# A two-layer hybrid decoder on one core: reordered work ahead of the first retrieval turn, the depthwise convolution on VectorE, and seven slots for rows of U

## The chip, the cores and the metric

One core of one Trainium2 chip runs the whole program in one launch. The metric is the device time of one execution in microseconds, here the median of the runs shown. All data is float32.

## The reference

Two layers act on x of 256 tokens by 1024. Each has two sub-layers with a post-norm residual, x <- LayerNorm(alpha x + (1 + gate) f(x (1 + scale) + shift)); scale, shift and gate come from silu(c) @ w_ada + b_ada, six vectors of 1024 per layer.

```python
proj = h @ w_in[l]                       # 1024 -> 1440, split into seven parts
o_mla  = mla_attention(...)              # 8 heads, low-rank q and kv, rotary key
o_conv = conformer_conv(conv_u, ...)     # GLU, depthwise conv over 31 taps, LayerNorm, silu, pointwise
o_swa  = swa_attention(...)              # window of 128, 4 query heads
mix = concatenate([o_mla, o_conv, o_swa]) @ w_o[l]
...
q = h @ w_pq                             # PEER: 8 heads, two halves of 128
s1, i1 = top_k(scores half 1, 16); s2, i2 = top_k(scores half 2, 16)
top_s, pos = top_k(all 256 sums, 16)     # 16 of 16384 experts per token and head
a = gelu(einsum('bqd,bqkd->bqk', xb, u_tab[e]))
y = einsum('bqk,bqkd->bqd', softmax(top_s) * a, v_tab[e])
```

The convolution is causal: for each of 256 channels, out[s] = b_dw + sum over k of h[s - 30 + k] w_dw[k].

## The kernel before

Tokens are in two blocks of 128, so there are four blocks of work, numbered m = 0 to 3 (two layers of two). Each block has eight turns, one per PEER head, and a turn has sixteen items: for item k, every one of the 128 tokens gathers its k-th row of U (4 KB each, one indirect DMA of 0.524 MB) and its k-th row of V. That makes 32 turns, 512 gathers of U and 512 of V, all issued by GpSimd in one order: U of item n + 16, then V of item n - 4.

Time is laid out by hand in **slots**. A slot is one item: slot 16 i + k is turn i, item k, and negative slots lie before the first turn. Each engine's program is a set of generators that yield the slot at which their next piece is due; `in_slot_order` (L193) merges them in slot order, and each engine's main loop runs its turn work and then everything due up to the present slot. Block m's mixing (projection, attention, convolution, output projection, norm) starts at slot BASE[m] = -140, 0, 132, 260, so that block 0's mixing lies before the first turn and each later one beside the turns of the block before. An engine does its work strictly in this order, so an early wait holds up all that is behind it.

What the change and the steps of the prediction touch:

- **U and V rows.** `ring` has UR = 6 slots for U and VR = 8 for V (L72, L235). `gather_u` (L653) waits until VectorE has used the row that was in its slot six items ago; `gather_v` (L665) waits for TensorE. VectorE's `product` (L1262, instruction L1268) multiplies a row of U by the token's own row and sums it; TensorE's `weigh` (L1707, L1721) adds rows of V into the output, weighted. Before the first turn the ring also holds pieces of w_ada, w_in and w_o.
- **Picks.** VectorE's `picks` (L1199) finds the sixteen experts of a turn in eight parts, one in each of the first eight slots of a turn, so that those slots are heavier than the last eight. The first gather waits for the picks of turn 0.
- **Query.** TensorE computes a turn's query (L1666), turns it (L1675) and computes the scores (L1685); ScalarE copies each out (L940, L945, L952).
- **Convolution.** ScalarE writes a diagonal matrix of one tap's weights (L903, `cdiag`, nine buffers) and TensorE multiplies the shifted input `hc` by it, adding in PSUM (L1609): 31 taps by 2 halves of the channels, 62 steps a block, three steps per slot from slot b + 31.2 on (b is BASE[m]). The bank "cv" is held from 31.2 to 53.3. VectorE then takes statistics (L1197), ScalarE normalises (L917) and applies silu (L921), TensorE does the pointwise product (L1623).
- **Modulation of layer 0.** w_ada is loaded in twelve chunks of 512 columns, two halves of 1 MB each (L500, L505). TensorE multiplies them (`products_of`, L1363), ScalarE copies the row (L718), TensorE turns it into columns (L1378).
- **Modulation of layer 1.** Chunks 0 to 6 are summed by VectorE (`summed`, L476: L486 for the first of eight, L491 for the others), at slots from SUM_START, and turned into columns by TensorE (L1397) at COLUMN_SLOT; chunks 7 to 11 are multiplied by TensorE at SECOND_SLOT (L1390) and their rows copied by ScalarE (L728). GpSimd waits for the sums of chunk 6 before the first gather, for the product of chunk 9 before the fifth, and for all columns before the first gather of V.
- **Loads.** SyncE issues all weights in slot order. A load waits until its buffer is free: `startup` (L544) loads chunks 4 and 5 of layer 0 (L553) ahead of the last two of the eight pieces of w_in (L556), then chunks 6 and 7. The pieces are win_load (L507).
- **End of block 0's mixing.** TensorE's output projection (L1577) is followed by VectorE's use of it (L1185, slot 74) and statistics (slot 75), the turning of sub-keys on TensorE (L1637, slots 75 and 76), ScalarE's norm (L704 to L708, slot 76.75), its turning (slot 77), the input of the query (L878).
- **Rowmax.** At slot b + 45 VectorE reduces the scores of all heads (L1151); ScalarE's exponentials (L843) wait for that and TensorE's turning of them (L1533, slot b + 48) waits for those.
- **hc** is cleared or shifted for a new block by VectorE (L1098) and ScalarE (L811), after all steps of the block before (`diag_used`).

## Time and profile before

| | |
|---|---|
| runs | 1712.57, 1715.56, 1716.38 us (median 1715.56) |
| the profiled execution's own time | 1710.71 us |
| its span | 1708.8 us |
| granted TensorE clock, mean | 0.856 |
| TensorE matmul busy | 1214.5 us, 71% |
| VectorE busy | 1063.2 us, 62% |
| GpSimd busy | 981.5 us, 57% |
| ScalarE busy | 412.9 us, 24% |

Busy time is the union of an engine's instructions. In views that list stretches, the DMA share is the mean busy share of sixteen DMA engines, so that a value just over 1 is a full one. In lists in order of time a row gives start, duration, engine, line and operation, and in brackets the idle time before it and what ended that. Work before about 200 us is that ahead of the first turn.

### The profile page before, as it was taken

Reading aid. Unit: us, or ns where it says so; the run is one execution under the profiler, and the core shown is the slowest. Engines: PE = TensorE matmul, PEld = TensorE weight load, DVE = VectorE, ACT = ScalarE, POOL = GpSimd, SP = SyncE. Lnnn points to the kernel's source line nnn. Section 1 sums busy time; section 2 is a strip of 40 time slices with the busy share of each in tenths; the row PEclk is TensorE's granted clock in tenths of the full one; section 3 lists DMA queues with packets and bytes.
Section 4 is the critical chain, followed back from the end, with each engine's and each line's share of the span. In section 5 each row is a group of like instructions: output and inputs, shape, how many; then the busy total and the mean of one; then the engine's idle time right before and its main releaser. Section 6 shows DMA issues by size and latency. Waiting matters only on the chain.

```text
span 1708.8 us, 16190 instructions
## 1 busy us (share of the span) xinstructions
PE 1214.5 (71%) x5018; PEld 544.5 (32%) x5018; DVE 1063.2 (62%) x3052; ACT 412.9 (24%) x1000; POOL 981.5 (57%) x1044
## 2 busy tenths in 40 slices
PE   6887749789766667798665567798866665666554
PEld 2465523355222222354221222355322221222111
DVE  0165486577666566577576566577766686667652
ACT  1362302454121012354031012355120020011000
POOL 2000166567666566567566566566766666667763
PEclk8997859999977779899988788899988887778789
DMA  9989999999999999999999999999999999999996
GB/s 364 342 307 352 344 400 405 405 404 409 407 398 405 410 395 403 404 403 388 404 402 406 410 391 403 405 394 342 409 405 405 405 405 407 406 408 409 410 409 235
DMA packets 217190, 667.12 MB, mean 390 GB/s; under 512 B 21586, under 2 KB 50611, under 8 KB 217106
## 3 DMA queue, kind: packets, MB, share of 16 engines
q0 software_dynamic: 148240, 538.63, 79.9%
q1 hardware_dynamic: 68866, 127.46, 20.2%
q8 instruction: 41, 0.67, 0.2%
q14 instruction: 43, 0.35, 0.1%
HBM read 664.97 MB, written 1.05 MB: 390 GB/s over the span
## 4 chain that ended last, share of the span: by engine, by line
DMA 48%; PE 18%; DVE 16%; POOL 9%; issue 6%; ACT 2%; SPq 1%; POOLq 0%; DVEq 0%; ACTq 0%
DMA ring<-in_u_tab,uidx 25%; DMA ring<-in_v_tab,vidx 17%; DVE ring L1268 6%; PE y L1721 6%; POOL ring L660 4%; POOL ring L672 4%; DMA wo<-in_w_ada 3%; PE qb L1666 2%; PE m L1609 2%; DMA ring<-in_w_ada 1%; PE m L1432 1%; PE m L1577 1%; DMA win<-in_w_in 1%; DVE junk L1244 1%; PE m L1363 1%
## 5 line engine op out<-in xcount | busy, mean ns | idle before, releaser
L1721 PE MATMUL y<-ring,place 128*32 128x512 f32 x2048 | 617.2, 731 | 394.4 <-DMA ring<-in_v_tab,vidx 357.2
L1268 DVE SCALAR_TENSOR_TENSOR ring<-ring,hp 128x1024 f32<-128x1024 f32 x512 | 620.9, 1217 | 426.3 <-DMA ring<-in_u_tab,uidx 408.5
L660 POOL DMA_INDIRECT ring<-in_u_tab,uidx x512 | 488.4, 954 | 512.9 <-DVE ring L1268 287.5
L672 POOL DMA_INDIRECT ring<-in_v_tab,vidx x512 | 483.2, 944 | 166.1 <-issue 143.6
L1721 PEld LDWEIGHTS y<-ring,place 128*32 128x32 f32 x2048 | 126.3, 122 | 704.4 <-issue 701.6
L1666 PE MATMUL qb<-wpq,hT 128*128 128x256 f32 x512 | 137.0, 407 | 8.1 <-DVE vidx L1289 4.9
L1666 PEld LDWEIGHTS qb<-wpq,hT 128*128 128x128 f32 x512 | 95.9, 199 | 77.9 <-issue 67.3
L903 ACT ACTIVATE cdiag<-cst,wdT 128x128 f32<-128x128 f32 x248 | 79.5, 391 | 61.2 <-PE m L1609 61.2
L1432 PE MATMUL m<-win,hT 128*128 128x480 f32 x186 | 86.9, 611 | 7.6 <-DMA win<-in_w_in 5.2
L958 ACT ACTIVATE gexp<-best,nbest 128x16 f32<-128x16 f32 x32 | 9.9, 308 | 260.0 <-DVE nbest L1235 259.9
L1609 PE MATMUL m<-cdiag,hc 128*128 128x128 f32 x496 | 71.8, 288 | 0.0
L1609 PEld LDWEIGHTS m<-cdiag,hc 128*128 128x128 f32 x496 | 64.3, 197 | 21.3 <-issue 18.4
L940 ACT COPY qrow<-qb 128x256 f32<-128x256 f32 x32 | 11.8, 369 | 196.2 <-PE qb L1666 196.2
L1577 PE MATMUL m<-wo,hT 128*128 128x512 f32 x112 | 55.1, 618 | 0.0
L1432 PEld LDWEIGHTS m<-win,hT 128*128 128x128 f32 x186 | 36.6, 207 | 51.3 <-issue 45.0
L964 ACT ACTIVATE gel<-dots 128x16 f32<-128x16 f32 x32 | 6.9, 216 | 177.5 <-DVE ring L1268 177.4
L1268 DVE DVE_READ_ACCUMULATOR ring<-ring,hp 128x1 f32 x512 | 42.4, 83 | 0.0
L1244 DVE TENSOR_TENSOR junk<-junk,cide 128x432 f32<-128x432 f32 x64 | 39.5, 617 | 2.2
L952 ACT COPY sc<-qb 128x256 f32<-128x256 f32 x32 | 11.8, 368 | 119.6 <-PE qb L1685 119.6
L1246 DVE TENSOR_REDUCE eidf<-junk 128x8 f32<-128x432 f32 x64 | 38.6, 603 | 2.2
L964 ACT ACT_TABLE_LOAD x31 | 39.8, 1283 | 0.5
L1242 DVE TENSOR_TENSOR junk<-posf,cst 128x432 f32<-128x432 f32 x64 | 38.8, 606 | 0.9 <-DVE modc L1038 0.3
(244 smaller groups left out, 1222.9 us busy)
## 6 DMA issues: line engine op xcount, KB each, us to landing
ring<-in_w_ada SPq DMA_DIRECT2D x34, 1024.0 KB, 11.6
wpq<-in_w_pq SPq DMA_DIRECT2D x28, 1024.0 KB, 16.5
win<-in_w_in SPq DMA_DIRECT2D x31, 720.0 KB, 13.1
wo<-in_w_ada SPq DMA_DIRECT2D x14, 1024.0 KB, 13.1
wo<-in_w_o SPq DMA_DIRECT2D x28, 512.0 KB, 9.7
ring<-in_u_tab,uidx POOLq DMA_INDIRECT x512, 14.1
ring<-in_v_tab,vidx POOLq DMA_INDIRECT x512, 14.2
ring<-in_w_o SPq DMA_DIRECT2D x4, 512.0 KB, 8.6
```

The costliest lines, as they stand in the source:

```text
L660: nc.gpsimd.indirect_dma_start(out=ring[:, n % UR, :], out_offset=None, in_=u_flat, in_offset=bass.IndirectOffsetOnAxis(ap=uidx[:, g % 2, ...
L672: nc.gpsimd.indirect_dma_start(out=ring[:, UR + n % VR, :], out_offset=None, in_=v_flat, in_offset=bass.IndirectOffsetOnAxis(ap=vidx[:, g ...
L903: f(cdiag[:, q % DIAGS, :], ident, ACT.Copy, scale=wdT[:, n, 1 + k:2 + k]).then_inc(s["diag_ready"], 1)
L964: f(gel[:, g % 2, :], dots[:, g % 2, :], ACT.Gelu).then_inc(s["gelu_out"], 1)
L1242: chain(v.tensor_tensor(eq, each(posf[:, cut], NCAND), over(iota_row, TOPK // 2), ALU.is_equal))
L1244: chain(v.tensor_tensor(eq, eq, over(cide[:, :], TOPK // 2), ALU.mult))
L1268: v.scalar_tensor_tensor(ring[:, n % UR, :], ring[:, n % UR, :], 1.0, HP[:, :], ALU.mult, ALU.mult, accum_out=dots[:, g % 2, k:k + 1]).the ...
L1432: e = mm(banks[n][:, 0:PROJ_N], hT[:, k, cut], win_w[slot][:, n * PROJ_N:(n + 1) * PROJ_N], start=k == 0, stop=k == KC - 1)
L1577: e = mm(banks[n][:, :], hT[:, k, cut], wo_w[slot][:, n * 512:(n + 1) * 512], start=j == 0, stop=j == KC - 1)
L1609: mm(conv[:, n * P:(n + 1) * P], hc[:, n, k:k + P], cdiag[:, q % DIAGS, :], start=False, stop=False).then_inc(s["diag_used"], 1)
L1666: e = mm(Q_BANK[:, 0:2 * PK], hT[:, k, t * P:(t + 1) * P], wpq_w[head_of(g) % 2][:, k, :], start=k == 0, stop=k == KC - 1)
L1721: e = mm(Y[n][lo:lo + QUAD, :], place[:, g % 2, run_of(k), :], ring[:, UR + (g * TOPK + k) % VR, n * 512:(n + 1) * 512], start=g % PH == 0 ...
```

## The change

Seven parts. (1) UR is 7: `ring` has fifteen slots and V's begin one further on. (2) The convolution goes to VectorE. For each half of the channels the first tap writes `conv` as a product plus the bias, and 30 further taps multiply and add in place; three steps per slot from b + 31.2 on, the halves alternating, each step waiting for the last one of its half. At b + 52.2 TensorE waits for `conv_made` and transposes the two halves into the bank "cv", which is held from there on only. `cdiag` and its two semaphores are gone. (3) SyncE loads chunk 5 of layer 0 behind the last two pieces of w_in. (4) The sums of chunk 6 move from slots 66 to 73 to slots 76 to 76.7. (5) The columns of chunks 3, 4 and 5 move from slots 75.2, 75.25 and 75.3 to 80, 80.1 and 80.2. (6) Chunks 7, 8 and 9 of layer 1 move from slots -37, -36 and -28 to -34.5, -33.5 and -29; the query's scores of turn 0 are made at slot -36 and copied at -35. (7) The waits before `hc` is refilled are on `conv_made`.

```diff
-UR = 6
+UR = 7
-DIAGS = 9
-SUM_START = ((34, 0.7), (45.1, 0.18), (46.6, 0.18), (48.1, 0.55), (54.95, 0.4), (58.5, 1.0), (66, 1.0))
+SUM_START = ((34, 0.7), (45.1, 0.18), (46.6, 0.18), (48.1, 0.55), (54.95, 0.4), (58.5, 1.0), (76, 0.1))
-COLUMN_SLOT = (53.36, 53.37, 57.6, 75.2, 75.25, 75.3, 100.9)
-SECOND_SLOT = {7: -37, 8: -36, 9: -28, 10: -21, 11: -12}
+COLUMN_SLOT = (53.36, 53.37, 57.6, 80, 80.1, 80.2, 100.9)
+SECOND_SLOT = {7: -34.5, 8: -33.5, 9: -29, 10: -21, 11: -12}
...
-                (TAP_SLOT, 53.3, "cv"), (36, 36.5, "hq0 hq1"), (37, 38, "hk0 hk1"), (39, 40, "s0 s1"),
+                (52.2, 53.3, "cv"), (36, 36.5, "hq0 hq1"), (37, 38, "hk0 hk1"), (39, 40, "s0 s1"),
...
-        cdiag = sb("cdiag", [P, DIAGS, P])
+        conv = sb("conv", [P, CC, P])
...
-                for k in range(4, 6):
-                    full(sp, ("ad", k - 4))
-                    ada_load(0, k)
+                full(sp, ("ad", 0))
+                ada_load(0, 4)
                 for k in range(WIN_SLOTS + 1, KC):
                     sp.wait_ge(s["win_used"], k - WIN_SLOTS)
                     win_load(0, k)
-                for k in range(6, 8):
+                for k in range(5, 8):
                     full(sp, ("ad", k - 4))
                     ada_load(0, k)
...
# VectorE
             def convolution(m, b):
+                done = [0] * CC
+                for j in range(CONV_STEPS):
+                    if j % TAP_STEP == 0:
+                        yield b + TAP_SLOT + j // TAP_STEP
+                    k, n = conv_step(j)
+                    if j == 0:
+                        taken(dve, ("glu", m))
+                        taken(dve, ("wd", m // TB * TB))
+                        chain.sync()
+                    to, rows_, tap = conv[:, n, :], hc[:, n, k:k + P], wdT[:, n, 1 + k:2 + k]
+                    if k == 0:
+                        chain(v.tensor_scalar(to, rows_, tap, wdT[:, n, 0:1], ALU.mult, ALU.add))
+                    else:
+                        dve.wait_ge(s["dve_chain"], done[n])
+                        e = v.scalar_tensor_tensor(to, rows_, tap, to, ALU.mult, ALU.add)
+                        if k < TAPS - 1:
+                            chain(e)
+                        else:
+                            e.then_inc(s["conv_made"], 1)
+                    done[n] = chain.n
                 yield b + 52.8
...
# TensorE
-                yield b + TAP_SLOT
-                conv = fill(("cv", m))
-                for j in range(CONV_STEPS):
...
+                yield b + 52.2
+                pe.wait_ge(s["conv_made"], CC * (m + 1))
+                bank = fill(("cv", m))
+                for n in range(CC):
+                    e = tr(bank[:, n * P:(n + 1) * P], conv[:, n, :], ident)
+                filled(e, ("cv", m))
```

## Rows read from the trace of the kernel before

**Rows 1.** The page's line on the sum of all DMA packets.

```profile
DMA packets 217190, 667.12 MB, mean 390 GB/s; under 512 B 21586, under 2 KB 50611, under 8 KB 217106
```

**Rows 2.** Busy time by stretch: start:end, width, engines, granted clock, DMA share, GB/s.

```profile
70.00:105.00 35.00, 33.11 (x249) 23.30 (x249) 16.20 (x41) 27.21 (x83) 0.00 (x0) 1.00 0.69 245
...
150.00:185.00 35.00, 22.70 (x105) 17.15 (x104) 10.04 (x17) 12.38 (x27) 0.00 (x0) 0.71 0.84 314
200.00:1120.00 920.00, 669.53 (x2689) 295.53 (x2686) 614.03 (x1827) 237.60 (x580) 581.08 (x613) 0.86 1.03 403
1680.00:1708.00 28.00, 12.61 (x54) 2.89 (x50) 6.84 (x11) 1.74 (x3) 6.55 (x7) 0.88 0.52 205
```

The engines in these rows are TensorE matmul, its weight loads, VectorE, ScalarE and GpSimd.

**Rows 3.** By stretch: tap slots of blocks 1, 2, 3; heavy half of block 3.

```profile
334.00:404.50 70.50, 63.85 (x374) 41.19 (x374) 60.02 (x191) 38.26 (x108) 44.93 (x47) 0.99 1.03 406
713.50:782.90 69.40, 60.91 (x327) 34.86 (x324) 55.09 (x181) 36.88 (x116) 43.75 (x46) 0.94 1.02 402
1098.40:1172.00 73.60, 63.05 (x323) 36.55 (x321) 58.68 (x184) 38.78 (x117) 43.85 (x46) 0.94 0.97 375
1145.00:1172.00 27.00, 21.45 (x116) 13.06 (x114) 24.74 (x80) 15.99 (x53) 14.46 (x16) 0.94 0.90 338
```

**Rows 4.** In order of time, 22 to 62 us: SyncE's issues, TensorE's projection.

```profile
23.91 22.73 SPq L505 DMA_DIRECT2D ring<-in_w_ada  x4
...
46.68 3.44 SPq L510 DMA_DIRECT2D win<-in_w_in  x2
...
60.40 1.97 PE L1432 MATMUL m<-win,hT 128*128 128x480 f32 x2 [5.23 <-DMA win<-in_w_in]
```

**Rows 5.** In order of time, 150 to 200 us: from output projection to first gather.

```profile
151.76 0.49 DVE L486 TENSOR_SCALAR ring<-ring,ccol 128x512 f32<-128x512 f32 x1 [5.81 <-DMA ring<-in_w_ada]
...
153.21 0.60 PE L1637 MATMUL m<-cst,win 128*128 128x128 f32 x4
...
157.77 1.28 DVE L1185 SCALAR_TENSOR_TENSOR rows<-rows,m 128x512 f32<-128x512 f32 x2
...
162.43 3.55 PE L1397 MATMUL y<-cst,place 128*128 128x1 f32 x16
...
167.58 1.28 ACT L704 ACT_TABLE_LOAD   x1
...
187.63 0.59 ACT L728 COPY rowbuf<-y 128x512 f32<-128x512 f32 x1 [3.02 <-PE y L1363]
...
188.11 0.38 ACT L952 COPY sc<-qb 128x256 f32<-128x256 f32 x1
...
199.09 1.02 POOL L660 DMA_INDIRECT ring<-in_u_tab,uidx  x1 [160.93 <-DVE uidx L1248]
```

**Rows 6.** Groups by line and shape: count, busy us, mean ns, idle before.

```profile
L903 ACT ACTIVATE cdiag<-cst,wdT 128x128 f32<-128x128 f32 x248 | 79.5, 391 | 61.2 <-PE m L1609 61.2
L1609 PE MATMUL m<-cdiag,hc 128*128 128x128 f32 x496 | 71.8, 288 | 0.0
...
L491 DVE SCALAR_TENSOR_TENSOR ring<-ring,ccol 128x512 f32<-128x512 f32 x35 | 26.3, 752 | 7.4 <-DMA ring<-in_w_ada 5.7
...
L1278 DVE SCALAR_TENSOR_TENSOR coef<-gel,ginv,gexp 128x16 f32<-128x16 f32 x32 | 7.6, 236 | 5.4 <-ACT gel L964 1.9
```

**Rows 7.** In order of time: runs of VectorE instructions, dependent and independent.

```profile
102.73 5.58 DVE L491 SCALAR_TENSOR_TENSOR ring<-ring,ccol 128x512 f32<-128x512 f32 x7
...
724.35 0.88 DVE L1296 TENSOR_TENSOR place<-cst,qb 128x128 f32<-128x128 f32 x4
```

**Rows 8.** Around block 3's rowmax: by stretch, then in order of time.

```profile
1156.00:1162.00 6.00, 1.51 (x12) 1.32 (x12) 5.89 (x32) 5.88 (x24) 2.80 (x3) 0.99 0.52 182
...
1151.72 0.93 POOL L660 DMA_INDIRECT ring<-in_u_tab,uidx  x1 [2.69 <-DVE ring L1268]
...
1152.20 3.34 DVE L1151 TENSOR_REDUCE rowmax<-rows 128x12 f32<-128x3072 f32 x1
...
1158.59 0.93 POOL L660 DMA_INDIRECT ring<-in_u_tab,uidx  x1 [4.70 <-DVE ring L1268]
```

More of the change, by code:

```diff
@@ L430, in build @@
         ln_in skr_in wpq_in0 wpq_in1 bank_full0 bank_full1 bank_full2 bank_out0 bank_out1 bank_out2 rms_sums rms_inverse rms_out
-        glu_ready rope_ready max_ready exp_out diag_ready diag_used conv_stats crow_out ln_stats xn_out h2T_out h_made
+        glu_ready rope_ready max_ready exp_out conv_made conv_stats crow_out ln_stats xn_out h2T_out h_made
         q_made q_out qT_made qT_out s_made s_out picks_ready gate_out idx_ready idx_spread idx_turned vidx_ready
@@ L808, in mixing @@
                 yield b + 29
+                if m:
+                    act.wait_ge(s["conv_made"], CC * m)
                 if t:
-                    act.wait_ge(s["diag_used"], CONV_STEPS * m)
                     chain(copy(hc[:, :, 0:PAD], hc[:, :, P:P + PAD]))
@@ L895, in convolution @@
                 cut = slice(t * P, (t + 1) * P)
-                def diagonals(j0, j1):
-                    for j in range(j0, min(j1, CONV_STEPS)):
-                        k, n = conv_step(j)
-                        q = CONV_STEPS * m + j
-                        if q >= DIAGS:
-                            act.wait_ge(s["diag_used"], q - DIAGS + 1)
-                        f(cdiag[:, q % DIAGS, :], ident, ACT.Copy,
-                          scale=wdT[:, n, 1 + k:2 + k]).then_inc(s["diag_ready"], 1)
-                yield b + 29.2
-                taken(act, ("wd", TB * l))
-                diagonals(0, TAP_STEP)
-                yield b + 30
-                diagonals(TAP_STEP, 2 * TAP_STEP)
-                for d in range(TAP_SLOTS - 2):
-                    yield b + TAP_SLOT + d + 0.1
-                    diagonals(TAP_STEP * (d + 2), TAP_STEP * (d + 3))
                 yield b + 53.2
@@ L1096, in mixing @@
                     if m:
-                        dve.wait_ge(s["diag_used"], CONV_STEPS * m)
+                        dve.wait_ge(s["conv_made"], CC * m)
                     chain(v.memset(hc[:, :, 0:PAD], 0.0))
@@ L1597, in convolution @@
                 t = m % TB
-                yield b + TAP_SLOT
-                conv = fill(("cv", m))
-                for j in range(CONV_STEPS):
-                    if j and j % TAP_STEP == 0:
-                        yield b + TAP_SLOT + j // TAP_STEP
-                    k, n = conv_step(j)
-                    q = CONV_STEPS * m + j
-                    if j == 0:
-                        taken(pe, ("glu", m))
-                        mm(conv[:, 0:CONV], ones[0:1, :], wdraw[0:1, :], start=True, stop=False)
-                    pe.wait_ge(s["diag_ready"], q + 1)
-                    mm(conv[:, n * P:(n + 1) * P], hc[:, n, k:k + P], cdiag[:, q % DIAGS, :],
-                       start=False, stop=False).then_inc(s["diag_used"], 1)
-                filled(mm(conv[:, 0:CONV], zero_row, any_row[:, 0:CONV], start=False, stop=True), ("cv", m))
+                yield b + 52.2
[4 more added lines that the diff above has]
+                filled(e, ("cv", m))
                 yield b + 54.2
```

## The prediction

> **What bounds the kernel now.** I read the page's DMA lines first. All the memory traffic, 667.12 MB, passes in 1708.8 us at a mean of 390 GB/s [rows 1]. From 200 to 1120 us the sixteen DMA engines are busy 1.03 of the time and move 403 GB/s, with TensorE busy 669.53 of 920 us, VectorE 614.03 and GpSimd 581.08 [rows 2]. So the stream of table rows is bound by DMA, and the change moves no bytes. Time can only come from stretches in which DMA idles: (1.03 - share) x width. Before the first turn these are 0.34 x 35 = 12 us between 70 and 105 us and 0.19 x 35 = 7 us between 150 and 185 us, 19 us together; at the end, 0.51 x 28 = 14 us from 1680 us on, which the change doesn't touch [rows 2]. Inside the stream, block 3 (1098 to 1172 us) loses 0.06 x 73.6 = 4.4 us; block 1 and block 2, at 1.03 and 1.02, lose under 1 us [rows 3].
>
> **Start, part one: chunk 5 goes behind the input weights.** The queue issues chunks 4 and 5 from 23.91 us and the last two pieces of w_in only at 46.68; TensorE then waits 5.23 us and goes on at 60.40 [rows 4]. One chunk is 2.1 MB, 5.2 us at 403 GB/s. The pieces come that much earlier, and so does all that hangs on the projection: -5 us on the path. The two DMA issues of chunk 5 are moved past two issues of w_in on SyncE's queue; its product is due only after the projection, so its later landing costs nothing (the cover is the projection's last two pieces; if it goes, TensorE waits for chunk 5 instead, up to the same 5 us).
>
> **Start, part two: sums and columns.** TensorE has finished the output projection by 153.21, where it turns keys, but VectorE stands 5.81 us before the sums of chunk 6, which start at 151.76, and takes up the result only at 157.77 [rows 5]. With those sums at slot 76, 4.5 us go. Sixteen column products take 3.55 us at 162.43, ahead of the last keys, and ScalarE's norm starts behind these at 167.58 [rows 5]; all 24 take 24/16 x 3.55 = 5.3 us. At slots 80 to 80.2 they stand between the turned norm and the first query, where ScalarE is writing the query's input: I take 3 us as covered by that, and 2.5 come back on the path. Gain: 3 us (if the cover is gone, none). Then ScalarE waits 3.02 us for chunk 8's product and copies its row in 0.59 before it copies the scores at 188.11 [rows 5]: with both chunks behind the scores, 3.6 us go, and some 0.4 of chunk 7's work on TensorE. Late next are the products of chunks 7 and 8 themselves, and the fifth gather, which waits for that of chunk 9, now due one slot earlier. Chain: 5 + 4.5 + 3 + 4 = 16 us, so the first gather leaves near 183 us instead of 199.09 [rows 5].
>
> These 16 us are not the gain. The bytes loaded before are the same and DMA is full for most of that time: the end moves only by the holes closed. The 12 us hole group is DMA waiting for buffers that TensorE's products and VectorE's sums free. Coming 5 us earlier, with the taps no longer among TensorE's instructions, closes some 9 of it; what stays is the wait for the first sums of chunk 1, now behind taps on VectorE. Of the 7 us, the wait of chunk 10's load for chunk 7's product mostly closes; the wait for the end of the output projection grows. I take 1 net. Prologue: -10 us, bounds 0 and -19.
>
> **The convolution.** TensorE loses 496 recorded passes of 288 ns, 71.8 us, and ScalarE loses 248 diagonals of 391 ns, 79.5 us [rows 6]; on TensorE come two transposes a block, under 1 us each by the same row. Neither engine bounds the stream (669.53 of 920 us busy) [rows 2], so this is worth nothing directly; it lets TensorE run ahead in blocks whose taps keep it at 61 to 64 of 69 to 74 us [rows 3]. VectorE gets 62 steps a block, each a multiply-add of 128 columns with a scalar per partition, two interleaved chains. No row has this form. Duration: the same operation takes 752 ns at 512 columns and 236 ns at 16 [rows 6], 1.04 ns a column, so 352 ns at 128. Upper end, if each waits for the one before: seven at 512 take 5.58 us, (5.58 - 0.75)/6 = 0.80 apart, 0.05 over the duration [rows 7]: 0.40 us. Lower end: four independent products of 128 columns in 0.88 us, (0.88 - 0.28)/3 = 0.20 apart [rows 7]. Each step waits for the one two back, (0.35 + 0.05)/2 = 0.20, so the lower row is the nearer; the scalar's fetch may add the 0.07 by which this form is longer. I take 0.24: 15 us a block, 60 in all, bounds 12 and 25 a block.
>
> The Trainium skill (VectorE: DVE Perf Modes, The DRAIN you can't avoid) says that a next operation does not start until the pipe is empty, waits or none; by that a step is its whole 0.35 us, 22 us a block. The trace contradicts it for independent operations [rows 7], and no row shows two interleaved chains; by this rule the time would be the third rival's, just over its threshold, about 1717.
>
> **Does VectorE keep up?** Demand in the three tap stretches is 60.02, 55.09 and 58.68 us busy of 70.50, 69.40 and 73.60 [rows 3]. Add 15: 75, 70 and 74. Block 1 overruns by 4.5 us, the others by about 0.5, but unevenly: the first eight slots of a turn hold the picks, and block 3's take 24.74 of 27.00 us already [rows 3]; 23 steps more, 5.5 us, make 30.2 us for some 22.6 us of DMA work (27.00 less the 4.4 lost). Lag: 7.6 us. The cushion is read at rowmax: GpSimd's gathers wait 2.69 and 4.70 us for VectorE, 7.4 together, and DMA idles 0.51 x 6 = 3.1 us between 1156 and 1162 [rows 8]. So six rows of U absorb 4.3 us. A seventh adds one slot, two rows of 0.524 MB at 403 GB/s, 2.6 us: 6.9. Block 3 would lose about 1 us in place of 4.4, and blocks 1 and 2 stay inside the cushion. I take -2 for all three, as a new wait remains: TensorE stands at slot 52.2 for conv_made, and behind it on its queue are the weighings of V and the next queries. Its V rows outlast that, eight of them. Bounds: -5 (all dips gone) and +15 (below). ScalarE's and VectorE's waits for conv_made before hc is refilled come a block later and cost nothing.
>
> **Sum.** -10 - 2 = -12 us against the profiled execution's own 1710.71 us (span 1708.8), so 1699. The three runs' median is 1715.56, 4.9 higher; against it the same gain gives 1703.5. A measurement tells about 0.2% here, 3.4 us.
>
> **Rivals.** (1) All holes close: the 19 us and the 5 us of dips. For it: 16 us of chain against 19 of holes. Against it: buffers freed by sums that now stand among taps. 24 us: 1691.5. (2) The holes only move: gathers start 16 us sooner but the loads of the second modulation wait for VectorE, whose sums now come among the taps. For it: VectorE is already busy 16.20 of 35 us between 70 and 105 us, and 15 us of taps fall on it and the next 20 us [rows 2]. Then 3 us of prologue remain and the blocks give nothing: 1712.5. (3) The other side: VectorE becomes the bound in the tap stretches. At 0.40 us a step the taps take 25 us a block. Lags: 60.02 + 25 - 70.50 = 14.5 in block 1, 10.7 in block 2, 58.68 + 25 - (73.60 - 4.4) = 14.5 in block 3; less the cushion of 6.9, losses of 8, 4 and 8, of which block 3 has 4.4 today: 15 us more. Ten of the 25 also fall on the sums before the first turn and take half of the 10 gained there: 1715.5 + 15 - 5 = 1725. It decides at about 0.33 us a step (20.5 us a block): lags 10, 6 and 10, losses of 3, 0 and 3, while the holes before the first turn, fed by VectorE, no longer close. For it: the waits on the own chain; against it: the independent products [rows 7]. That the change does not do what it says is possible only for the seventh row: if GpSimd waits for idx or for V instead, it is idle SBUF, and the cushion is 4.3 us; that costs some 4 us, 1707.
>
> **How the numbers follow.** Forecast 0.62 (with the idle seventh row in it), all holes close 0.14, holes only move 0.12, VectorE bound 0.12. Forecast: 1703. Its own spread, prologue -4 to -15, is 1697 to 1710. To leave out 2 in 10, the range takes in most of rival 1 and all of rival 2 and cuts rival 3: 1691 to 1718. Faster by over 0.2% (under 1712.1): 0.62 + 0.14 less the forecast's thin upper edge plus a little of rival 2, 0.77. Within 0.2%: most of rival 2 and rival 3 near its threshold, 0.12. Slower: 0.11.
>
> **What would show it.** First gather near 183 us; the wait for w_in near 55 us and under 1 us; a 5 us slice without DMA traffic (the one at 85 us, inside the 12 us) gone; the tap's group on VectorE at 62 x 4 with a mean near 350 ns, six in a run spanning 1.5 us; VectorE's busy share near 66 to 68%; GB/s between 1150 and 1172 us' counterpart near 380 rather than 338. Wrong, if steps stand 0.33 us or more apart, if the tap stretches fall below 1.00 DMA share in blocks 1 and 2, or if the holes before the first gather still sum to over 15 us.

## The result, and the profile after

The changed kernel takes **1725.26 us** (median of 6 runs, 1721.05 to 1726.74), the kernel before 1713.67 (6 runs beside them): the ratio is 1.0067, 95% interval [1.0056, 1.0079]. It is slower by 11.6 us; forecast were 12 us the other way. All ratios and intervals here and below use fast runs alone; of all runs one was slow, a run of the kernel with late chunks and six slots (1878 us, at a granted clock of 0.56). The profiled execution has a span of 1723.5 us against 1708.8, and a mean granted clock of 0.82 against 0.856.

The page of the kernel after: the engines' busy time, and the sum of all DMA packets (that of before is [rows 1]).

```profile
PE 1188.0 (69%) x4514; PEld 499.5 (29%) x4514; DVE 1126.9 (65%) x3300; ACT 338.0 (20%) x752; POOL 990.3 (57%) x1044
...
DMA packets 217186, 667.05 MB, mean 387 GB/s; under 512 B 21586, under 2 KB 50611, under 8 KB 217106
```

The work moved as described: ScalarE has 75 us less, VectorE 64 us more, the bytes are the same. They pass at 387 GB/s instead of 390, so DMA idles more than before. Where, is told by the busy time by stretch of the kernel after (columns as in [rows 2]):

```profile
70.00:105.00 35.00, 24.99 (x124) 13.84 (x124) 30.29 (x88) 11.96 (x40) 0.00 (x0) 0.70 0.93 331
105.00:140.00 35.00, 23.13 (x122) 18.59 (x123) 24.89 (x55) 9.43 (x17) 0.00 (x0) 0.59 0.99 347
140.00:155.00 15.00, 14.42 (x46) 6.96 (x44) 7.59 (x11) 1.65 (x3) 0.00 (x0) 1.00 0.59 201
155.00:185.00 30.00, 23.79 (x137) 17.32 (x134) 16.38 (x60) 12.07 (x28) 0.00 (x0) 0.77 1.04 393
...
250.00:275.00 25.00, 18.69 (x72) 8.68 (x66) 13.17 (x25) 5.53 (x13) 7.17 (x8) 0.66 0.62 224
...
389.60:428.30 38.70, 34.10 (x190) 20.07 (x190) 34.73 (x111) 17.70 (x38) 25.73 (x27) 0.91 0.98 372
```

The stretch of 250 to 275 us in the kernel before, which has no such pause:

```profile
250.00:275.00 25.00, 24.96 (x90) 11.71 (x90) 14.94 (x29) 6.97 (x15) 17.17 (x19) 0.85 1.03 409
```

Before the first gather the big hole between 70 and 105 us is nearly closed (share 0.93 for 0.69), and a new one has opened between 140 and 155 (0.59, 0.44 x 15 = 7 us; the kernel before had 0.92 there). Behind the first gather, where DMA was full, there is now a pause of 0.41 x 25 = 10 us. It is this second one that the sum did not have.

Since every item gathers two rows of the table and DMA bounds the stream, the start of an item is a clock of its own. This table, worked out from the starts of VectorE's `product` in the two profiled executions, says how far behind (+) or ahead (-) of the kernel before the changed one stands (the differences are taken before rounding):

| at | before, us | after, us | difference |
|---|---|---|---|
| first gather | 199.1 | 185.5 | -13.6 |
| item 16 | 236.2 | 224.0 | -12.2 |
| item 32 | 281.3 | 282.8 | +1.4 |
| item 48 (block 1's tap slots begin) | 334.0 | 337.1 | +3.0 |
| item 80 | 420.6 | 428.3 | +7.7 |
| item 176 (block 2's) | 713.5 | 719.7 | +6.2 |
| item 208 | 804.4 | 807.6 | +3.2 |
| item 304 (block 3's) | 1098.4 | 1103.1 | +4.7 |
| item 352 | 1237.2 | 1248.2 | +10.9 |
| end | 1708.8 | 1723.5 | +14.7 |

So 13.6 us are won at the start and lost again by item 32; blocks 1 and 3 cost 5 and 6 us more, block 2 gives 3 back. The last 4 us, behind item 352, have no cause that I can name. A second trace of the same kernel (the changed kernel run again, below) has 1 us there, and several kernels below 1 to 4, so that they are no more than what traces of one kernel differ by. The trace of the kernel before is also a quick one (1710.71 us against a median of 1713.67), which makes up 3 of the 14.7 us at the end.

**The pause behind the first gather.** The chain that ended last in the kernel after (start, width, what; its longest pieces) shows what takes its time there: loads of w_ada, one behind the other.

```profile
181.30 21.79 DMA wo<-in_w_ada
205.54 24.64 DMA wo<-in_w_ada
232.64 23.85 DMA wo<-in_w_ada
...
1185.22 10.14 PE m L1549 x48
```

And in order of time: TensorE, then GpSimd (start, duration, line, in brackets the idle time before).

```profile
249.14 1.94 PE L1365 MATMUL m<-wo,ccol 128*32 128x512 f32 x8 [10.10 <-DMA wo<-in_w_ada]
256.54 1.93 PE L1365 MATMUL m<-wo,ccol 128*32 128x512 f32 x8 [5.46 <-DMA wo<-in_w_ada]
...
261.09 3.63 PE L1715 MATMUL y<-ring,place 128*32 128x512 f32 x8
...
248.63 0.94 POOL L658 DMA_INDIRECT ring<-in_u_tab,uidx  x1 [0.30 <-issue]
264.98 0.99 POOL L670 DMA_INDIRECT ring<-in_v_tab,vidx  x1 [15.42 <-PE y L1715]
```

TensorE stands 10.10 and 5.46 us for the two halves of chunk 11 of layer 0 (the last chunk of the first modulation, in the buffers of w_o, due at slot 2.5), and its first weighing of V follows only at 261.09. By then all eight slots for V are full, GpSimd can issue nothing for 15.42 us, and DMA runs dry. In the kernel before the same two chunks take the same serial loads (19.55 and 20.62 us in its chain, from 204.59), but its gathers start at 199 and DMA stays full to the end of them (1.03). In the changed kernel these two loads start at 205.54, no earlier than before, and take 24.64 and 23.85 us: 12 and 28 gathers had been issued when they were, against 5 and 16 in the kernel before. By bringing the gathers 14 us forward and not these loads, the change uncovers them.

### The profile page after: what moved, and what is told of

It is laid out like the page before. It is cut to its first block, busy times and chain, and to the rows that moved or that the text cites. A ratio compares the mean times of both kernels' runs of the same rounds, so it can differ in the third digit from the quotient of the medians.

```text
span 1723.5 us, 15184 instructions
## 1 busy us (share of the span) xinstructions
PE 1188.0 (69%) x4514; PEld 499.5 (29%) x4514; DVE 1126.9 (65%) x3300; ACT 338.0 (20%) x752; POOL 990.3 (57%) x1044
## 4 chain that ended last, share of the span: by engine, by line
DMA 47%; PE 18%; DVE 13%; POOL 9%; issue 5%; ACT 1%; SPq 0%; POOLq 0%; DVEq 0%; ACTq 0%
DMA ring<-in_v_tab,vidx 26%; DMA ring<-in_u_tab,uidx 17%; PE y L1715 8%; DVE ring L1270 5%; POOL ring L670 5%; POOL ring L658 4%; DMA wo<-in_w_ada 4%; PE m L1579 2%; PE qb L1660 2%; DVE conv L1191 2%; PE m L1549 1%; PE m L1434 1%; PE y L1399 1%; PE m L1345 1%; DVE junk L1246 1%
## 5 line engine op out<-in xcount | busy, mean ns | idle before, releaser
L1715 PE MATMUL y<-ring,place 128*32 128x512 f32 x2048 | 634.1, 749 | 398.1 <-DMA ring<-in_v_tab,vidx 358.2
L670 POOL DMA_INDIRECT ring<-in_v_tab,vidx x512 | 490.5, 958 | 311.6 <-PE y L1715 180.2
L1434 PE MATMUL m<-win,hT 128*128 128x480 f32 x186 | 83.3, 590 | 2.4 <-ACT hT L754 2.4
L1191 DVE SCALAR_TENSOR_TENSOR conv<-hc,wdT,conv 128x128 f32<-128x128 f32 x240 | 70.0, 347 | 0.0
L1020 DVE TENSOR_TENSOR modc<-m,colT 128x4 f32<-128x4 f32 x12 | 1.9, 160 | 63.7 <-PE m L1380 63.7
L1365 PE MATMUL m<-wo,ccol 128*32 128x512 f32 x80 | 17.4, 982 | 30.3 <-DMA wo<-in_w_ada 30.2
```

Source lines behind the costliest of these rows:

```text
L670: nc.gpsimd.indirect_dma_start(out=ring[:, UR + n % VR, :], out_offset=None, in_=v_flat, in_offset=bass.IndirectOffsetOnAxis(ap=vidx[:, g ...
L1191: e = v.scalar_tensor_tensor(to, rows_, tap, to, ALU.mult, ALU.add)
L1434: e = mm(banks[n][:, 0:PROJ_N], hT[:, k, cut], win_w[slot][:, n * PROJ_N:(n + 1) * PROJ_N], start=k == 0, stop=k == KC - 1)
L1715: e = mm(Y[n][lo:lo + QUAD, :], place[:, g % 2, run_of(k), :], ring[:, UR + (g * TOPK + k) % VR, n * 512:(n + 1) * 512], start=g % PH == 0 ...
```

## The experiments

Three theories were put to the test. A: the start gives back what it wins, by the pause behind the first gather. B: the taps cost more on VectorE than they free on TensorE. C: part of B comes not from VectorE but from TensorE, whose clock falls where the taps have left it. An expectation below also speaks of B', which is B beside C: the loss is VectorE's own time.

Eighteen kernels ran in five jobs, each job on another chip. Ratios are to the kernel before in the same job. On the chips of the first job (before: 1781.07) and of the last (1773.14) DMA itself is less regular, so all ratios are read within a job and those two chips stand by themselves; on the others before took 1712.3 to 1712.8. Where two kernels of different jobs are compared below, that is said, and the difference carries the noise of both ratios, about 0.15 to 0.25%. The next two rows are one kernel (late chunks, below) between 1200 and 1600 us, first on a regular chip, then on the last job's: the share is full in both, the bytes per second are not.

```profile
1200.00:1600.00 400.00, 265.88 (x892) 92.79 (x892) 277.85 (x811) 53.64 (x103) 278.73 (x295) 0.80 1.03 406
```

```profile
1200.00:1600.00 400.00, 254.85 (x896) 90.63 (x894) 268.04 (x789) 54.94 (x106) 265.55 (x279) 0.79 1.01 387
```

### The parts of the change, one by one

**Reordered start only** (parts 3 to 6; taps stay on TensorE, six slots for U), on two chips:

```diff
-SUM_START = (..., (66, 1.0))
-COLUMN_SLOT = (53.36, 53.37, 57.6, 75.2, 75.25, 75.3, 100.9)
-SECOND_SLOT = {7: -37, 8: -36, 9: -28, 10: -21, 11: -12}
+SUM_START = (..., (76, 0.1))
+COLUMN_SLOT = (53.36, 53.37, 57.6, 80, 80.1, 80.2, 100.9)
+SECOND_SLOT = {7: -34.5, 8: -33.5, 9: -29, 10: -21, 11: -12}
...
-                for k in range(4, 6):
-                    full(sp, ("ad", k - 4))
-                    ada_load(0, k)
+                full(sp, ("ad", 0))
+                ada_load(0, 4)
...
-                for k in range(6, 8):
+                for k in range(5, 8):
```

> The kernel before with the reordering alone (chunk 5 behind the input weights, sums of chunk 6, columns of chunks 3 to 5, chunks 7 to 9 of layer 1 moved); the taps stay on TensorE and U has six slots. Theory A (chunks 10 and 11 of layer 0 are loaded one after the other behind earlier gathers, and TensorE stands before their products with V's slots full): the start loses again what it gains, the DMA pause near 255 us is there, time within 5 us of before (1713.7), rather above it. Theory B (the loss is VectorE's, in the tap stretches): no taps on VectorE, so the gain at the start shows whole, some 7 to 10 us faster than before.

Measured 0.9979 [0.9946, 1.0011], not clear of noise.

> Reordering alone, again, now beside the changed kernel. Theory A (serial loads of chunks 10 and 11 behind the earlier gathers): DMA's pause of 7 to 10 us near 255 us again, time 0.998 to 1.003 of before. Theory B (the loss is all VectorE's): 0.994 to 0.996 of before.

Measured 0.9966 [0.9953, 0.9978], -4.7 us by the medians (1707.55 to 1712.29). The first gather leaves at 176.8 us, 22 us earlier than before; by item 32 only 8 of them are left, by item 80 six. The reordering works and is mostly given back behind the first gather. The ratio itself lies between what A and B had named, so it is the trace that decides for A. TensorE stands for chunk 11 as in the changed kernel, and DMA has its pause (the columns of the second row are those of [rows 2]):

```profile
238.59 1.93 PE L1362 MATMUL m<-wo,ccol 128*32 128x512 f32 x8 [10.86 <-DMA wo<-in_w_ada]
250.00:275.00 25.00, 25.00 (x93) 10.50 (x92) 17.20 (x34) 8.49 (x17) 15.40 (x17) 0.91 0.74 272
```

**Taps on VectorE only**, which is the changed kernel with the diff above undone; in the first of the three runs with six slots, in the others with seven:

```diff
-UR = 7
+UR = 6
```

> The kernel before with the convolution on VectorE alone, six slots of U, old order ahead of the first turn. Theory A: the start is that of before but for taps among the sums; no pause near 255 us; 1716 to 1719, the loss of blocks 1 and 3 growing by some 4 us. Theory B: the whole loss or more is here, 1724 to 1728.

Measured 0.9973 [0.9948, 0.9998]. Both theories had expected a loss; the chip was one of the two irregular ones.

> As the one with the taps on VectorE alone, with the seventh slot of U. Both theories: a slot is worth one item of lag in the tap stretches, 2 to 3 us less than with six slots. If U's seventh slot is idle, no difference.

Measured 0.9905 [0.9879, 0.9931].

> Taps on VectorE and seven slots, old order ahead of the first turn. Theory A: no pause near 255 us; faster than the changed kernel by 3 to 6 us, since the reordering gains less than the pause costs. Theory B: as slow as the changed kernel or slower by the 7 us that the start gained.

Measured 1.0056 [1.0035, 1.0077], +10.2 us. The same kernel wins 1% on the irregular chip and loses 0.6% on a regular one. It has no pause behind its first gather (199.2 us); blocks 1 and 3 take 2 and 7 us longer than before. Theory A expected this kernel 3 to 6 us faster than the changed one; it is as slow, as theory B said, because A's estimate left out what the taps cost. Beside taps on VectorE the reordered start with its pause is worth nothing.

**The changed kernel itself**, beside these on a regular chip:

> The changed kernel unaltered, beside the kernel before, as the yardstick for the others of this job: the kernel before took 1781 us in the last job against 1714 in the first, so ratios hold only within a job. If the first job's ratio holds everywhere, 1.007 of before. If irregular DMA latency makes the seventh slot worth more, as the 0.9905 of taps with seven slots against 0.9973 with six suggests, below 1.00 where before is slow, and 1.007 where before is near 1714.

Measured 1.0056 [1.0035, 1.0078], +9.4 us. The parts alone are -4.7 and +10.2; their sum is 5.5, together they give 9.4. The difference of 3.9 us is less than the noise of the three ratios together (some 5 us), so that no extra price of the combination is shown. This is also a second trace of the changed kernel: its first gather leaves at 180.5 us where the first trace had 185.5. Differences of up to 5 us ahead of the first gather can therefore be one kernel's own spread.

### The pause: when the last chunks are multiplied

The products of chunks 10 and 11 of layer 0 give the gate of the second sub-layer, which is used at slot 131. They can be made later:

```diff
-        at = BASE[0] + c if c < 4 else (-2, 2.5)[c - 10]
+        at = BASE[0] + c if c < 4 else (2.5, 24)[c - 10]
```

In the changed kernel:

> The changed kernel with the products of chunks 10 and 11 of layer 0 at slots 2.5 and 24 in place of -2 and 2.5; they are first used at slot 131. Theory A: TensorE no longer stands before V's first rows, the DMA pause near 255 us (12 us with no traffic) goes, 9 to 12 us faster than the changed kernel, 1714 to 1716. Theory B: no more than 2 us faster than the changed kernel's 1725.3.

Measured 0.9866 [0.9831, 0.9902], on the first, irregular chip.

> The changed kernel with chunks 10 and 11 at slots 2.5 and 24. Theory A: 0.993 to 0.995 of the changed kernel in the same job (9 to 12 us). Theory B: within 2 us of the changed kernel.

Measured 0.9998 [0.9988, 1.0008]: 9.7 us less than the changed kernel beside it, as theory A had said (9 to 12). Its trace, 235 to 260 us by stretch, and GpSimd there:

```profile
235.00:260.00 25.00, 17.27 (x65) 7.96 (x65) 13.60 (x35) 5.32 (x13) 15.15 (x17) 0.93 1.03 401
```

```profile
245.40 0.94 POOL L658 DMA_INDIRECT ring<-in_u_tab,uidx  x1 [0.30 <-issue]
247.09 0.93 POOL L670 DMA_INDIRECT ring<-in_v_tab,vidx  x1 [0.75 <-PE y L1715]
```

DMA is full, and the wait of 15.42 us has become one of 0.75. The same two lines in the reordered start alone:

> The kernel before, reordered, with chunks 10 and 11 at slots 2.5 and 24; taps on TensorE, six slots of U. Theory A: the pause of 8.3 us near 255 us goes as it did with the late chunks, 0.990 to 0.993 of before, the fastest of all; if the pause was a property of seven slots alone, 0.9966 as the reordering alone.

Measured **0.9925 [0.9909, 0.9942]**, 1699.88 us. And in the kernel before with nothing else changed, beside the last one once more:

> The kernel before with chunks 10 and 11 of the first layer multiplied later (slots 2.5 and 24), all else as it was. Theory A (the pause of DMA after the first gather exists only because the first gather now leaves earlier): nothing to win, since the kernel before has no such pause, so 0.998 to 1.001. Rival (late products are worth 7 us in any order, for instance because TensorE is freed of them in the prologue): 0.996. If it comes out at 0.9925, reordering the start is worth nothing at all once these products are late.

Measured 1.0006 [0.9997, 1.0015].

> The fastest kernel so far once more on another chip: the reordered start with the late products, taps on TensorE, six slots for rows of U. It was 0.9925 [0.9909, 0.9942]; expected 0.991 to 0.994. It is the partner of the late products alone.

Measured 0.9928 [0.9915, 0.9941], 1700.46 us.

That settles the pause. Late products are worth nothing where the gathers leave at 199 us (1.0006), and 0.4% or 7 us where they leave at 177 to 180 (0.9966 to 0.9925, from two jobs, the latter confirmed by 0.9928); the reordering is worth 0.3% without and 0.7%, 12 us, with them. Neither is enough alone.

### What is left: the convolution on VectorE

**Six slots** in the late kernel:

```diff
-UR = 7
+UR = 6
```

> The changed kernel with the late chunks and six slots of U in place of seven. If the seventh slot is worth one item of lag in each tap stretch: 4 to 8 us slower than with seven, 1.003 to 1.005 of before. If it is worth nothing on a chip without irregular DMA: 0.9998.

Measured 1.0019 [0.9998, 1.004]. Against seven slots (0.9998 [0.9988, 1.0008], another job) that is 0.2%, 3.6 us, on a regular chip, and not clear of noise, since the intervals touch. On the irregular chip, within one job, the slot was worth a clear 0.7% (0.9973 to 0.9905).

**No taps** (this kernel leaves out 29 of the 31 taps, on every engine):

```diff
                     k, n = conv_step(j)
+                    if 0 < k < TAPS - 1:
+                        continue
```

> The changed kernel with the late chunks 10 and 11, and with 29 of the 31 taps left out on VectorE (first and last tap alone are computed); TensorE's and ScalarE's work as in the changed kernel. Theory B' (in the blocks beside turns the loss is VectorE's time for 62 steps at 0.29 us each): block 3's items 304 to 352 take at most 139 us as before or less, against 144 to 147; the time falls by 9 to 14 us against the late chunks' 0.9998 of before, to 0.992 to 0.995. Theory C (the loss is TensorE's: with its taps gone it idles, its clock falls to 0.5 to 0.7 just where it has to catch up): hardly any gain, 0.998 or more.

Measured 0.9921 [0.9905, 0.9938]. Against the late kernel (0.9998, another job) 0.77%, 13 us: that is the price of the taps on VectorE. B' had foretold 0.992 to 0.995, C 0.998 or more. With all its taps on TensorE and six slots the reordered late kernel (0.9925, the same job) is as fast within the noise as this one, which computes almost none: there they cost nothing that can be measured.

**Products that nobody reads**, 62 a block on TensorE in the tap slots, written to the bank that the transposes overwrite:

```diff
+                yield b + TAP_SLOT
+                bank = fill(("cv", m))
+                for j in range(CONV_STEPS):
+                    if j and j % TAP_STEP == 0:
+                        yield b + TAP_SLOT + j // TAP_STEP
+                    n = j % CC
+                    mm(bank[:, n * P:(n + 1) * P], ident, ident, start=True, stop=True)
                 yield b + 52.2
```

> The changed kernel with the late chunks, and on TensorE 62 products of 128x128 per block at the slots where its taps stood, into the bank that the transposed convolution overwrites (nothing reads them). Theory C (clock): the granted clock in block 3's tap stretch comes back to 0.95 or more and the time falls by 3 to 6 us, 0.996 to 0.998. Theory B': the clock comes back and the time stays or grows, 0.999 to 1.003.

Measured 0.9961 [0.9949, 0.9974]: more work on TensorE made the kernel 0.37%, 6 us, faster than the late one (0.9998, another job). By the two traces 3.6 us of it lie ahead of the first gather (182.9 for 186.5), which is within one kernel's own spread, and 2.8 in block 3. Then in block 3 alone, and in blocks 0 to 2 alone (`if m == 3`, `if m < 3` around the product):

> The changed kernel with late products, and unread products of TensorE in the tap slots of block 3 alone. Theory C (TensorE's clock falls where the taps have left it, and only in block 3 does TensorE then bound the stretch): all of the 6.3 us that fillers in every block gave come from here, 0.996 to 0.9975. Rival (the fillers help through all blocks alike, or through the prologue): a quarter of it, 0.9985 to 1.000.

Measured 0.9988 [0.9979, 0.9997].

> The same with the unread products in blocks 0, 1 and 2 and none in block 3. Theory C: no better than without fillers, 0.999 to 1.001. Rival: three quarters of the gain, 0.997.

Measured 0.9988 [0.998, 0.9997]. Against the late kernel of another job each half gives 0.1%, 1.7 us, which is not clear of noise and less than half of 6; theory C's claim that all of it comes from block 3 fell. The last pair should fix the size, both on one chip:

> The changed kernel with the late products, without fillers, once more, so that it stands beside the fillers on one chip: 0.9990 to 1.0005 (it was 0.9998 [0.9988, 1.0008]).

Measured 0.9871 [0.9824, 0.9918].

> The same with unread products in the tap slots of all four blocks, once more. Theory C with its size of 6.3 us: 0.996. If the two halves (block 3 alone, blocks 0 to 2 alone: 1.7 us each) simply add, 3.4 us in all: 0.9978 to 0.998. If what differed was only from where the first gather left, which moves by some us from one run of the same kernel to the next, no more than 0.999.

Measured 0.9878 [0.9837, 0.9919]. That chip was an irregular one, and on it the fillers give nothing that can be measured. The size stays open: 6 us by one comparison across two jobs, 3.4 by the sum of the halves, nothing on the irregular chip.

The mechanism, though, can be read in block 3. Items 304 to 352 of six kernels by stretch: before, after, late, late with fillers in blocks 0 to 2, late with fillers in block 3, no taps. One row each.

```profile
1098.40:1237.20 138.80, 120.73 (x595) 65.42 (x591) 103.60 (x301) 54.81 (x146) 90.22 (x96) 0.97 0.99 384
```

```profile
1103.10:1248.20 145.10, 117.37 (x469) 56.47 (x465) 119.84 (x364) 35.83 (x84) 92.35 (x95) 0.85 0.97 372
```

```profile
1094.70:1238.70 144.00, 115.91 (x469) 56.40 (x465) 119.87 (x364) 35.83 (x84) 92.17 (x95) 0.89 0.97 373
```

```profile
1089.00:1234.60 145.60, 116.36 (x469) 56.10 (x465) 119.86 (x363) 35.85 (x84) 93.00 (x95) 0.88 0.97 370
```

```profile
1096.10:1236.10 140.00, 120.11 (x593) 64.75 (x589) 119.88 (x363) 35.76 (x84) 93.42 (x96) 0.97 1.00 386
```

```profile
1083.30:1221.50 138.20, 111.04 (x468) 52.20 (x465) 104.68 (x305) 35.85 (x84) 91.11 (x97) 0.90 1.00 387
```

The three with taps on VectorE and no fillers there take 144 to 146 us, that with fillers 140, at the clock of before (0.97), and the one without taps 138. So of some 6 us that the taps cost in block 3, 4 go with fillers on TensorE and 2 stay with VectorE. TensorE in order of time in the kernel after, then GpSimd:

```profile
1184.57 0.44 PE L1604 MATMUL m<-cst,conv 128*128 128x128 f32 x2 [2.87 <-DVE conv L1191]
1184.84 0.38 PE L1669 MATMUL qb<-cst,qrow 128*128 128x128 f32 x2
1185.06 6.89 PE L1549 MATMUL m<-vrows,win 128*128 128x64 f32 x32
1191.74 3.62 PE L1549 MATMUL m<-vs,win 128*128 128x64 f32 x16
1195.29 3.61 PE L1715 MATMUL y<-ring,place 128*32 128x512 f32 x8
...
1199.17 0.94 POOL L670 DMA_INDIRECT ring<-in_v_tab,vidx  x1 [6.24 <-PE y L1715]
```

And in the kernel with fillers in block 3:

```profile
1177.63 0.44 PE L1612 MATMUL m<-cst,conv 128*128 128x128 f32 x2 [2.17 <-DVE conv L1191]
1177.90 0.38 PE L1677 MATMUL qb<-cst,qrow 128*128 128x128 f32 x2
1178.12 3.68 PE L1549 MATMUL m<-vrows,win 128*128 128x64 f32 x32
1181.64 1.95 PE L1549 MATMUL m<-vs,win 128*128 128x64 f32 x16
1183.52 1.91 PE L1723 MATMUL y<-ring,place 128*32 128x512 f32 x8
```

In both TensorE stands for `conv_made`, 2.87 and 2.17 us. Behind it come 48 products of the attention with the values, due in one piece, and then the weighing of V. In the changed kernel the 48 take 10.5 us and the weighing 3.61; with fillers 5.6 and 1.91, as in the kernel before. GpSimd finds V's eight slots full in the first case and waits 6.24 us; in the second it never waits for TensorE there. The granted clock of that stretch, first in the late kernel (which has the same picture as the changed one, with a wait of 6.24 us too), then with fillers in block 3:

```profile
1175.00:1190.00 15.00, 14.70 (x64) 11.95 (x65) 8.79 (x19) 3.63 (x5) 6.66 (x8) 0.54 0.85 319
```

```profile
1176.00:1188.80 12.80, 10.67 (x82) 8.62 (x84) 11.67 (x26) 5.66 (x11) 9.46 (x11) 1.00 0.98 351
```

At 0.54 TensorE is at the lower of its two levels (1.2 GHz) nearly all the time though it is busy for 14.70 of 15 us; at 1.00 it is at the upper (2.4 GHz). In the changed kernel it had been busy 23.5 of the 32.2 us ahead of its slow stretch, and then stood.

What takes the clock down is not the missing work alone. The kernel without taps has as little work on TensorE, but `conv` is ready when TensorE comes to it, so that there is no wait, and the same products run as fast as before:

```profile
1162.21 0.44 PE L1606 MATMUL m<-cst,conv 128*128 128x128 f32 x2
1162.70 3.68 PE L1551 MATMUL m<-vrows,win 128*128 128x64 f32 x32
```

And fillers alone do not hold it up. In block 2 of the kernel with fillers everywhere TensorE stands 3.91 us for `conv_made`, and its 24 products of that block take 5.2 us, as in the changed kernel (3.90 and 5.2), where before and without taps they take 2.8. In block 1 the changed kernel waits only 0.49 us, and its 48 take 5.6. In block 3 the fillers also shorten the wait: 0.60 and 2.17 us with them, 2.45 to 3.04 without (changed, late, taps alone, fillers in blocks 0 to 2). The late kernel on the two irregular chips, without fillers, waits 1.98 and 2.03 us, and its 48 take 5.8 and 8.8. So the slow stretch belongs to the wait for VectorE, on an engine that had little to do before it; how much of it is the wait and how much the missing work, these runs do not separate.

## Why the prediction was wrong

**The start.** Forecast: chain 16 us shorter, first gather near 183, 10 us of holes closed. The first gather leaves at 185.47 (180.5 in the second trace). In [rows 5]' terms, the kernel after:

```profile
162.35 3.55 PE L1399 MATMUL y<-cst,place 128*128 128x1 f32 x16
165.76 6.45 PE L1660 MATMUL qb<-wpq,hT 128*128 128x256 f32 x16
...
151.75 1.44 DVE L1167 SCALAR_TENSOR_TENSOR rows<-rows,m 128x512 f32<-128x512 f32 x2 [6.89 <-PE m L1579]
...
174.48 0.37 ACT L934 COPY sc<-qb 128x256 f32<-128x256 f32 x1 [0.80 <-PE qb L1679]
```

- Chunk 5, w_in: right. The last pieces are used at 54.78 without a wait; it was 60.40 after 5.23.
- Sums of chunk 6: the wait is gone, but VectorE takes up the output projection at 151.75, 6 us earlier than before, where the first two steps had 9.5. Here the prediction left something out. With the taps still on TensorE the same order ends the projection by 143.8; with them on VectorE by 152.3, as TensorE's next instruction shows. The reason is TensorE's longest wait between 60 us and the first gather, which no kernel with its taps on TensorE has:

```profile
119.93 0.69 PE L1604 MATMUL m<-cst,conv 128*128 128x128 f32 x2 [6.61 <-DVE conv L1191]
```

It is `conv_made`, in block 0. The taps stand among VectorE's sums, and the last two of them end at 119.9 behind sums of w_ada. The kernel without taps waits there too, since its last tap stands behind the same sums, but is through at 112.0. The prediction priced this wait for the three blocks beside turns only, and the new place of the taps before the first turn at nothing but "what stays" of a 12 us hole. In DMA's share over 70 to 177 us the price shows as 0.92 (changed) and 0.91 (late) against 0.99 (reordered alone, and no taps); the hole at 140 to 155 us by itself proves little, as the kernel without taps has it as well (0.66). The no-tap kernel's first gather is at 177.2, those of three traces with the taps on TensorE and the new order at 176.8, 179.1 and 180.0, those of three with the taps on VectorE and the new order at 185.5, 180.5 and 186.5: 5.5 us by the means, with a spread as large. This price only shows once the start is reordered; in the old order the first gather stayed at 199.2 with taps on VectorE.
- Columns: the scores' way back, a query that starts 1.8 us behind its input (165.76 for an input turned by 164.0), is about the 2.5 taken. Chunks 7 and 8: right, the scores are copied at 174.48 instead of 188.11, and nothing stands before them.
- Net: the share over 70 to 185 us rose from 0.87 to 0.93, 0.06 x 115 = 7 us. Ten were forecast, with bounds 0 and 19.

**The step that failed** is the sum's silence on what follows the first gather. "Late next are the products of chunks 7 and 8 themselves, and the fifth gather": the next late thing was chunk 11 of the *first* layer, whose loads stood in the chain of before (19.55 and 20.62 us), just covered. A chain that is shortened ahead of a fixed chain uncovers the latter. It took back 9.7 us, as the late kernel beside the changed one shows. Rival 2, holes that only move, described this half of what happened, but looked for it ahead of the first gather.

**The taps' size** was nearly right. In order of time, VectorE of the kernel after: nine steps in a row between blocks of other work, then three in the stream; and the step's group (count, busy us, mean ns).

```profile
92.74 2.44 DVE L1191 SCALAR_TENSOR_TENSOR conv<-hc,wdT,conv 128x128 f32<-128x128 f32 x9
95.10 1.75 DVE L1133 TENSOR_REDUCE rowmax<-rows 128x12 f32<-128x1536 f32 x1
...
348.10 0.87 DVE L1191 SCALAR_TENSOR_TENSOR conv<-hc,wdT,conv 128x128 f32<-128x128 f32 x3
349.00 0.09 DVE L1220 MATCH_VALUE_LOAD topi<-top,sc 128x8 f32 x1
```

```profile
L1191 DVE SCALAR_TENSOR_TENSOR conv<-hc,wdT,conv 128x128 f32<-128x128 f32 x240 | 70.0, 347 | 0.0
```

The duration is 347 ns (352 forecast). Nine steps take 2.36 us up to the next instruction, 0.26 each; three take 0.90, 0.30 each. The forecast was 0.24, within bounds of 0.20 and 0.40, and below the 0.33 from which the third rival was to decide. VectorE's whole busy time rose by 63.7 us, 16 a block (15 forecast), its share is 65%, just under the 66 to 68% named. The traffic in block 3's heavy half, foretold near 380 GB/s, is 340 (1150.6 to 1182.8 us; 338 before). Yet none of the three signs of being wrong came: steps stay under 0.33 us, the tap stretches of blocks 1 and 2 have shares of 1.01 and 1.03, and the holes before the first gather sum to some 12 us. The signs watched the terms of the sum; the pause behind the first gather and the wait of block 0 for `conv_made` lay outside them. The rule that was weighed, of the Trainium skill (VectorE: DVE Perf Modes, The DRAIN you can't avoid), would have made it 0.35 a step; at 0.26 it does not hold here, and the same paragraph of the page says, in a sentence that the prediction passed over, that a next operation which isn't held starts earlier.

**What VectorE does to the blocks** was too rosy nonetheless. Six slots were said to absorb 4.3 us and seven 6.9, and the three blocks to gain 2. They lose: block 1 has a share of 0.98 over 389.6 to 428.3 us, block 3 0.97 over 145 us where it had 0.99, and with no taps at all 1.00. Taps cost 13 us over the whole kernel (no taps against late; by the two traces 9 of it ahead of the first gather, 5 in block 1, 6 in block 3, and 3 come back in block 2 and some more behind). The seventh slot, reckoned at 2.6 us, gave 3.6, which is not clear of noise on a regular chip; that it is no idle room is shown on the irregular one.

**TensorE's relief "is worth nothing directly; it lets TensorE run ahead".** This sentence was wrong. Nothing let TensorE run ahead; in blocks 0, 2 and 3 it now waits for VectorE (`conv_made`; 6.61, 3.90 and 2.87 us), and behind the waits of blocks 2 and 3 it works at about half the clock. "Its V rows outlast that, eight of them": they did not, by 6.24 us in block 3, since behind the wait stand 48 products and a weighing at 1.2 GHz, 14 us in place of 7.5. In block 1, where the wait is 0.49 us, 5 us are lost all the same; that part is VectorE's own time.

**The two failed terms add up.** With the taps left on TensorE and the two late products, the reordered start gains 12 us (0.9925 and 0.9928), which happens to be the whole forecast. Taps on VectorE with seven slots take these 12 back (0.9925 to 0.9998), and the pause takes 9.7: about +10, where +9.4 and +11.6 were measured.

The third rival named the measured time, 1725, with a chance of 0.12, by a step price of 0.40 that was not met: its number was right by luck. None of the four cases held the one that happened, a start that gives back what it won while the taps cost 10 us or more at 0.26 a step.

## What to carry to other kernels

When a chain ahead of a steady stream is shortened, list everything with a fixed latency that was covered by its old length, the loads of the first turns above all, and move the users of those too: here two numbers turned a gain of 0.3% into one of 0.7%, the fastest kernel of the study but for the one that leaves out its taps (reordered start, late chunks, taps on TensorE, six slots: 1699.88 us, 0.9925). Before work is taken from an engine that is not the bound, look at what stands in one piece behind it on that engine and at the clock it would run at then; where another engine has to wait for the one that takes the work, that wait costs time long before its busy share looks full (VectorE stood at 65% here, and the taps cost 13 us). Price a term at every place where it occurs: the wait for `conv_made` was priced in three blocks and left out in the fourth.

## What was not expected of the hardware

- With 62 products a block gone from TensorE, and a wait of 2.9 us for VectorE in front, the granted clock of what follows in block 3 falls by nearly half: 0.54 over 15 us in which the engine was busy for 14.70 (in the late kernel, behind a wait of 3.04), and 32 products of 64 columns take 6.89 us instead of 3.68. With unread products put back, and a wait of 2.17, it is 1.00; with neither taps nor a wait the 32 take 3.68 as well. The Trainium skill (TensorE: Matmul & The Clock Gate, Part 1) says that the clock follows how busy the engine has been lately. Within the two rows it looks the other way round, as the busier stretch has the lower clock; the trace agrees only for the time ahead of them, where the engine had stood.
- Two interleaved chains of dependent multiply-adds of 128 columns on VectorE start 0.26 us apart (nine in a row) at a duration of 0.347 each.
- The second load of a pair of 1 MB each, issued beside the row gathers, takes 24.6 and 23.9 us to land in the kernel after (12 and 28 gathers issued by then), 19.6 and 20.6 in the one before (5 and 16).
- Chips differ more than the changes do: 1712 and 1781 us for one program; 406 and 387 GB/s at a full share on a regular chip and on the last job's; and the taps on VectorE with seven slots lose 0.6% on one and win 1% on another.
